# Two-layer decoder trunk on one core: the second layer's z turned by VectorE in 32x32 blocks, and a new walk of its output product

## The reference, cut to what matters

```
def conformer_mixer(hn, w_in, b_in, w_dw, b_dw, ln_g, ln_b, w_out, b_out):
    proj = hn @ w_in
    ab = proj[..., :2 * CONV_WIDTH] + b_in
    z = proj[..., 2 * CONV_WIDTH:]
    a, g = jnp.split(ab, 2, axis=-1)
    u = a * jax.nn.sigmoid(g)
    u = depthwise causal convolution of u over rows, 31 taps, + b_dw
    u = jax.nn.silu(layer_norm(u, ln_g, ln_b))
    return (u * jax.nn.silu(z)) @ w_out + b_out
```

## Time and profile before

| what | value |
|---|---|
| median of 3 runs | 853.53 us (853.16 to 853.54) |
| profiled execution, its own time | 853.52 us |
| its span in the trace | 851.5 us |
| busy: PE, DVE, ACT, POOL | 840.6, 654.5, 427.7, 337.7 us |
| granted TensorE clock, mean | 0.995 of full |
| read from memory | 156.94 MB, 187 GB/s over the span |

### The profile page before, as it was taken

One profiled execution on the slowest core, in us unless ns is written; L12 is line 12 of the kernel. 1 busy time (PEld: TensorE's weight loads), 2 busy tenths in 40 slices (PEclk: granted clock), 3 DMA queues, 4 the chain that ended last, 5 costly groups with the idle time before them and its releaser, 6 DMA issues.

```text
span 851.5 us, 12154 instructions
## 1 busy us (share of the span) xinstructions
PE 840.6 (99%) x3909; PEld 698.0 (82%) x3909; DVE 654.5 (77%) x1143; ACT 427.7 (50%) x592; POOL 337.7 (40%) x169
## 2 busy tenths in 40 slices
PE   8999999999999999999999999999999999999996
PEld 6888888888888888888888788888888888888884
DVE  4688678876889688877656629999999999566555
ACT  5744544454444644454455575445444554574441
POOL 0343005500441004500000298888888878772000
PEclk9999999999999999999999999999999999999998
DMA  9956556655666556645655465555555546556532
GB/s 325 300 158 206 162 168 197 195 153 167 191 200 194 154 157 198 216 148 200 208 189 196 146 198 195 176 177 195 194 169 181 196 152 197 194 208 239 196 98 99
DMA packets 97509, 159.49 MB, mean 187 GB/s; under 512 B 3300, under 2 KB 38468, under 8 KB 97092
## 3 DMA queue, kind: packets, MB, share of 16 engines
q1 hardware_dynamic: 97284, 158.97, 57.7%
q10 hardware_dynamic: 192, 0.08, 0.0%
HBM read 156.94 MB, written 2.10 MB: 187 GB/s over the span
## 4 chain that ended last, share of the span: by engine, by line
PE 97%; issue 1%; DMA 0%; DVE 0%; ACT 0%; DVEq 0%; POOLq 0%; POOL 0%; ACTq 0%
PE acc L419 29%; PE acc L421 29%; PE acc L420 29%; PE X L429 2%; PE acc L404 1%; PE acc L406 1%; PE acc L405 1%; PE acc L485 1%; PE acc L500 1%; PE X L550 1%; DMA ident<-in_identity 0%; PE X L559 0%; PE X L544 0%; PE X L543 0%; PE X L560 0%
## 5 line engine op out<-in xcount | busy, mean ns | idle before, releaser
L772 ACT ACTIVATE w_hi<-raw 128x1024 fp32r<-128x1024 f32 x282 | 298.9, 1061 | 359.8 <-PE acc L421 359.3
L419 PE MATMUL acc<-w_hi,xT_hi 128*128 128x512 f32 x864 | 339.6, 393 | 0.0
L421 PE MATMUL acc<-w_hi,xT_lo 128*128 128x512 f32 x864 | 336.6, 390 | 0.0
L420 PE MATMUL acc<-w_lo,xT_hi 128*128 128x512 f32 x864 | 336.2, 389 | 0.0
L1058 DVE TENSOR_TENSOR w_lo<-raw,w_hi 128x1024 fp32r<-128x1024 f32 x182 | 243.8, 1350 | 95.5 <-ACT w_hi L772 93.5
L1490 POOL TENSOR_TENSOR w_lo<-raw,w_hi 128x1024 fp32r<-128x1024 f32 x100 | 243.0, 2436 | 49.1 <-ACT w_hi L772 48.8
L421 PEld LDWEIGHTS acc<-w_hi,xT_lo 128*128 128x128 f32 x864 | 162.2, 188 | 34.0
L419 PEld LDWEIGHTS acc<-w_hi,xT_hi 128*128 128x128 f32 x864 | 162.3, 188 | 32.9 <-DVE xT_lo L1077 0.3
L420 PEld LDWEIGHTS acc<-w_lo,xT_hi 128*128 128x128 f32 x864 | 162.4, 188 | 32.6
L1315 DVE SCALAR_TENSOR_TENSOR X<-u_pad,taps,X 128x256 f32<-128x256 f32 x464 | 182.6, 480 | 0.0
L1453 POOL TENSOR_TENSOR small<-small 128x1 f32<-128x1 f32 (+1 forms) x7 | 4.3, 616 | 231.3 <-DVE small L1261 124.0
(11 more groups left out here) (150 smaller groups left out, 731.6 us busy)
## 6 DMA issues: line engine op xcount, KB each, us to landing
raw<-in_w_in SPq DMA_DIRECT2D x78, 1024.0 KB, 5.3
raw<-in_w_in SPq DMA_DIRECT2D x66, 512.0 KB, 4.4
raw<-in_w_out SPq DMA_DIRECT2D x32, 1024.0 KB, 5.0
gpost<-in_post_g SPq DMA_DIRECT2D x2, 1024.0 KB, 4.6
xrow<-in_x SPq DMA_DIRECT2D x4, 256.0 KB, 5.5
raw<-in_w_in SPq DMA_DIRECT2D x4, 256.0 KB, 4.8
xrow<-in_x SPq DMA_DIRECT2D x2, 512.0 KB, 9.5
bout<-in_b_out SPq DMA_DIRECT2D x1, 1024.0 KB, 7.0
```

Of the source, the lines that this page charges most:

```text
L419: nc.tensor.matmul(a, hi[:, k, rows], w_hi[:, slot, i], start=(k == 0), stop=False)
L420: nc.tensor.matmul(a, hi[:, k, rows], w_lo[:, slot, i], start=False, stop=False)
L421: last = nc.tensor.matmul(a, lo[:, k, rows], w_hi[:, slot, i], start=False, stop=(k == KT - 1))
L772: nc.scalar.activation(w_hi[:, slot], raw[:, u % LOADS, 2 * half:2 * half + 2], ACT.Copy).then_inc(hi_ready[slot], 1)
```

## The change

- `gate_T` and `GATE_AT` are gone. DVE turns z_row1 into a new tile `zT` in SBUF with `turn_gate`: 4 steps of 4 block transposes for each of 4 blocks. They are placed by hand among the statistics, the normalising and the gates.
- `gate` becomes one instruction of 128x1024 per block that reads cT and zT.
- The output product walks `OUT1_ORDER`: column blocks 0 and 1 over parts 0 to 3, then by turns parts 4 and 5, then 6 and 7, then blocks 2 and 3. A part is two k tiles, so vT block 2 is first needed at slice 8 and block 3 at slice 12. Bias, gain and squares of blocks 0 and 1 move with it.
- `final_high` of the four blocks stands after ACT's slices 0, 2, 5, 9 in place of 0, 2, 4, 6 (`FINAL_AT`).
- POOL makes the low parts of slices 0 to 9 in place of 0 to 7 (`OUT1_POOL`).
- `zT` takes the place of c_row; the post gain and the output bias are loaded into the place of xT_lo, once the z product is done, in place of that of z_row1.

```diff
--- before.py
+++ after.py
@@ -54,7 +54,6 @@
 NVEC = 5 * KT
 ROOT_AT = 27
 STAT_AT = 25
-GATE_AT = (26, 28, 30)
 ROWS_AT = (7, 9, 11, 23)
 LEAD = 2
 
@@ -71,6 +70,12 @@
 OUT0_ORDER = tuple([(0, i) for i in range(6)] + [(1, i) for i in range(6)] + [(0, 6), (0, 7), (1, 6), (1, 7)]
                    + [(n, i) for n in (2, 3) for i in range(SLICES)])
 OUT0_LAST = (13, 15, 23, 31)
+OUT1_ORDER = tuple([(n, i) for n in (0, 1) for i in range(4)] + [(n, k + i) for k in (4, 6) for n in (0, 1)
+                                                              for i in (0, 1)]
+                   + [(n, i) for n in (2, 3) for i in range(SLICES)])
+OUT1_LAST = (13, 15, 23, 31)
+OUT1_POOL = 10
+FINAL_AT = (0, 2, 5, 9)
 TURN_Q, TURN_K = 15, 24
 SCORES_AT = 26
 DW_ROWS = TAPS * KT // 4
@@ -114,8 +119,9 @@
         c_row = at("c_row", B, [P, MT, D])
         z_row1 = at("z_row1", B + 16 * KB, [P, MT, D])
         y1 = at("y1", B, [P, MT, D])
-        gpost1 = at("gpost1", B + 16 * KB, [P, D])
-        bout = at("bout", B + 24 * KB, [P, D])
+        zT = at("zT", B, [P, KT, SEQ])
+        gpost1 = at("gpost1", A + 16 * KB, [P, D])
+        bout = at("bout", A + 24 * KB, [P, D])
         Dr = 144 * KB
         q_row = at("q_row", Dr, [P, MT, NCOL])
         k_row = at("k_row", Dr + 4 * KB, [P, MT, NCOL])
@@ -376,10 +382,11 @@
                 for j in range(4):
                     load(S_Z, n, 8, j, w_in1[0], n * NCOL + 2 * D)
             for j in range(16):
-                load(S_OUT1, 0, 32, j, w_out1[0], (j // 4) * NCOL)
+                n, part = OUT1_ORDER[2 * j]
+                load(S_OUT1, 0, 32, j, w_out1[0], n * NCOL, part // 2)
                 if j == 5:
 
-                    sp.wait_ge(zT_done, NG)
+                    sp.wait_ge(w_used[RING - 1], rounds(S_OUT1, 0, 0, -1))
                     sp.dma_start(gpost1[:], post_g[1:2].to_broadcast([P, D])).then_inc(bcast1_in, 16)
                     sp.dma_start(bout[:], b_out[0:1].to_broadcast([P, D])).then_inc(bcast1_in, 16)
             ov = out.rearrange("b (m p) n -> p (b m) n", p=P)
@@ -699,15 +706,6 @@
                                                 start=True, stop=True)
                 last.then_inc(stat_ready, 1)
 
-            def gate_T(n):
-
-                pe.wait_ge(rows_out, 28 + n + 1)
-                if n:
-                    pe.wait_ge(t_ready, n)
-                for b in range(2):
-                    last = pair_T(z_row1, X[2 + b], 4 * n + 2 * b)
-                last.then_inc(zT_done, 1)
-
 
             for s in range(4 * SLICES):
                 if s % SLICES == 0:
@@ -719,19 +717,16 @@
                     conv_rows(ROWS_AT.index(s))
                 if s == STAT_AT:
                     statistics_wide()
-                if s in GATE_AT:
-                    gate_T(GATE_AT.index(s))
 
 
             for s in range(4 * SLICES):
-                if s % SLICES == 0:
-                    acc_free(32 + s // SLICES)
-                if s < SLICES and s % 2 == 0:
-                    pe.wait_ge(vlo_ready, s // 2 + 1)
+                n, part = OUT1_ORDER[s]
+                if part == 0:
+                    acc_free(32 + n)
+                if n == 0 and part % 2 == 0:
+                    pe.wait_ge(vlo_ready, part // 2 + 1)
                 if s < 4 * SLICES - RING:
-                    slice_products(S_OUT1, 0, 0, s, vT_hi, vT_lo)
-                if s == 1:
-                    gate_T(NG - 1)
+                    slice_products(S_OUT1, 0, 0, s, vT_hi, vT_lo, (n, part))
 
             def last_products(m):
 
@@ -1033,14 +1028,14 @@
 
             for s in range(4 * SLICES):
                 high(S_OUT1, 0, 0, s)
-                if s in (0, 2, 4, 6):
-                    final_high(s // 2)
+                if s in FINAL_AT:
+                    final_high(FINAL_AT.index(s))
                 if s == 3:
                     block_rows(S_Z, 0, 0, 31, z_row1[:, :, 3 * NCOL:4 * NCOL], rms[2], ACT.Silu)
                 if s in (1, 3):
                     affine_silu(2 + s // 2)
-                if s % SLICES == 4 and s > SLICES:
-                    out1_squares(s // SLICES - 1)
+                if s in (18, 20, 28):
+                    out1_squares((18, 20, 28).index(s))
             out1_squares(NG - 1)
 
 
@@ -1331,7 +1326,8 @@
                         conv_tap(h * 2 + c, c, k, h * per_pair + 2 * k - 1 + c)
 
 
-            for n in range(NG):
+            def row_stats(n):
+
                 for m in range(MT):
                     if n == NG - 1:
                         dve.wait_ge(cR_done, MT * n + m + 1)
@@ -1340,6 +1336,19 @@
                         dve.wait_ge(c_ready, MT * n + m + 1)
                         rows = c_row[:, m, n * NCOL:(n + 1) * NCOL]
                     nc.vector.bn_stats(bn[:, m, n], rows).then_inc(bn_ready, 1)
+
+            def turn_gate(n, steps):
+
+                if steps[0] == 0:
+                    dve.wait_ge(rows_out, 28 + n + 1)
+                for a in steps:
+                    turn(zT[:, 4 * n:4 * n + 4], z_row1[:, :, n * NCOL:(n + 1) * NCOL], a, zT_done)
+
+            for n in range(NG - 1):
+                row_stats(n)
+            dve.wait_ge(bn_ready, MT * (NG - 1))
+            turn_gate(0, (0, 1))
+            row_stats(NG - 1)
             dve.wait_ge(bn_ready, MT * NG)
             for m in range(MT):
                 nc.vector.bn_aggr(mv[:, m], bn[:, m]).then_inc(mv_ready, 1)
@@ -1358,11 +1367,9 @@
             def gate(n):
 
                 dve.wait_ge(silu_ready, n + 1)
-                dve.wait_ge(zT_done, n + 1)
-                for b in range(2):
-                    part = cT[:, 4 * n + 2 * b:4 * n + 2 * b + 2]
-                    last = nc.vector.tensor_tensor(part, part, X[2 + b][:].rearrange("p (t r) -> p t r", t=2), ALU.mult)
-                last.then_inc(t_ready, 1)
+                dve.wait_ge(zT_done, 4 * (n + 1))
+                c = cT[:, 4 * n:4 * n + 4]
+                nc.vector.tensor_tensor(c, c, zT[:, 4 * n:4 * n + 4], ALU.mult).then_inc(t_ready, 1)
 
             def final_low(n):
 
@@ -1370,17 +1377,24 @@
                 nc.vector.tensor_tensor(vT_lo[:, 4 * n:4 * n + 4], cT[:, 4 * n:4 * n + 4],
                                         vT_hi[:, 4 * n:4 * n + 4].bitcast(f32), ALU.subtract).then_inc(vlo_ready, 1)
 
+            turn_gate(0, (2, 3))
+            turn_gate(1, (0,))
             normalise(0)
             normalise(1)
+            turn_gate(1, (1, 2))
             gate(0)
             normalise(2)
+            turn_gate(1, (3,))
             gate(1)
             final_low(0)
             normalise(3)
+            final_low(1)
+            turn_gate(2, range(4))
             gate(2)
-            final_low(1)
+            turn_gate(3, (0,))
+            final_low(2)
+            turn_gate(3, (1, 2, 3))
             gate(3)
-            final_low(2)
             final_low(3)
 
             def out1_biased(n, m):
@@ -1391,7 +1405,7 @@
                     else:
                         dve.wait_ge(row1_done, 1)
                 else:
-                    dve.wait_ge(w_used[RING - 1], rounds(S_OUT1, 0, 0, 8 * n + 7))
+                    dve.wait_ge(w_used[OUT1_LAST[n] % RING], rounds(S_OUT1, 0, 0, OUT1_LAST[n]))
                 if n == 0:
                     dve.wait_ge(bcast1_in, 32)
                 c = slice(n * NCOL, (n + 1) * NCOL)
@@ -1403,13 +1417,14 @@
                 c = slice(n * NCOL, (n + 1) * NCOL)
                 nc.vector.tensor_tensor(yg1[:, m, c], y1[:, m, c], gpost1[:, c], ALU.mult).then_inc(yg_ready, 1)
 
-            for s in range(SLICES, 4 * SLICES):
+            for s in range(OUT1_POOL, 4 * SLICES):
                 low(S_OUT1, 0, 0, s)
-                if s % SLICES == 3:
+                if s in (17, 19, 27):
+                    n = (17, 19, 27).index(s)
                     for m in range(MT):
-                        out1_biased(s // SLICES - 1, m)
+                        out1_biased(n, m)
                     for m in range(MT):
-                        out1_gained(s // SLICES - 1, m)
+                        out1_gained(n, m)
             mean_but_last(30, 4)
             out1_biased(NG - 1, 0)
             out1_gained(NG - 1, 0)
@@ -1504,7 +1519,7 @@
                 if s == ROOT_AT:
                     inverse_root(rstd, var_eps, m_half, var_ready, 1, rstd_ready)
                 low(S_Z, 0, 0, s)
-            for s in range(SLICES):
+            for s in range(OUT1_POOL):
                 low(S_OUT1, 0, 0, s)
             for m in range(MT):
                 inverse_root(rms[3][:, m:m + 1], mean_sq[:, m:m + 1], m_half[:, m:m + 1], ms_ready, 5 + m, rms_ready)
```

## The result

The changed kernel takes 854.71 us (median of 11 runs, 853.25 to 856.81) against 853.45 us before (11 runs): the ratio is 1.0023, with a 95% interval of 1.0015 to 1.0031. The forecast was 854.4. The profiled execution took 854.35 us, its span is 852.6.

The account below looks back on a forecast made before the run. PE, busy 840.6 of 851.5 us, was taken to bound the kernel; -3.56 (bursts) + 3.4 (slice 0) + 0.7 (slice 6) + 0.4 (clock) = +0.9 gave 854.4 us, range 850.3 to 856.4.

Parts of the forecast that it names:

- The bursts: Four bursts of z transposes taken off PE around the start of the output product, 0.89 us each: -3.56 us.
- The wait at slice 0: Output product's start: PE waits for the first vT_lo, which DVE makes after POOL's low part: +3.4 us.
- The hidden work: DVE's turns (1.8 us each) before the statistics, gates, moved loads and new walk: mostly no cost to PE.
- These two cost nothing and save 2.1: POOL making the low parts of output product slices 8 and 9: no cost, 2.1 us saved.
- The wait at slice 6 and the clock: Output product: PE waits 0.7 us for POOL's slice 6 low part; a clock fall adds 0.4 behind it.
- I take L = 1.1: Loss from the clock's fall around the slice 0 wait: 1.1 us, of which slice 6's wait absorbs 0.7.
- -0.2 plus the larger of L and 0.7: Whole change against the kernel before: the sum for a given clock loss L, +3.2 us with L = 2 x 1.7.
- Rival 1: After the slice 0 wait the low clock lasts double or comes twice: 855.9 to 856.7 us, chance 0.20.
- Rival 2: DVE's turns take 1.9 us or more each, so slices 0 and 6 come later: 855.0 to 856.0, chance 0.11.
- Rival 3: Gate and vlo don't lose their turn to POOL; only 0.5 us wait at slice 0: 850.5 us, chance 0.19.

Follow-up runs that it names:

- e4: Changed kernel with z block 0 turned by TensorE in one burst and DVE's turns of blocks 1 to 3 rearranged; 850.48 us, ratio 0.9969 to the kernel before.
- e2: Changed kernel with z turned by TensorE again in four bursts and the gate reading PSUM, all else kept; 853.46 us, ratio 1.0001 to the kernel before.
- e3: Changed kernel with POOL's low part of output product slice 2 made to wait for DVE's first vT_lo; 851.93 us, ratio 0.9985 to the kernel before.
- e8: As e3, with POOL waiting ahead of slice 1, twelve POOL low parts, DVE's turns reordered, silus and final highs moved; 852.29 us, ratio 0.9991 to the kernel before.
- e6: Changed kernel with POOL making the low parts of eight output product slices instead of ten; 857.97 us, ratio 1.0057 to the kernel before.
- run b: Second of three repeat profiles of the unedited changed kernel; 857.31 us.
- e5: Changed kernel with the old walk of the output product and final highs after slices 0, 2, 4, 6; 863.87 us, ratio 1.0128 to the kernel before.
- runs a and c: First and third of three repeat profiles of the unedited changed kernel; 853.15 and 854.56 us.
- e1: Changed kernel with 13 idle products on TensorE ahead of slice 0 of the output product; 854.02 us, ratio 1.0007 to the kernel before.

## Why the prediction was right

Forecast were +0.9 us and 854.4. The medians differ by 1.3 us and R by 1.5; the mean of the 11 runs is 1.9 above that of before, because five of them form an upper group (855.93 to 856.81).

**The bursts** (-3.56): right. e4 saves three of them and its R falls by 2.7, e2 puts them back and nothing remains.

**The wait at slice 0** (+3.4): right in size, place and cause. 3.42 with the restart; the chain on DVE came within 0.1 us of the forecast at vT_lo. Of these 3.4 us about 2.2 are POOL's turn at the lock; the other 1.26, which e3 leaves, go when no turn stands between normalise 0 and the first vT_lo (e4). POOL was ahead of vT_lo by 0.11 us, as forecast (0.1), and the prediction itself says that this could have fallen the other way; it came out alike in every profile that has this order.

**The hidden work:** turns at 1.81 us, two of them free before the statistics, gates at 1.24, 1.40, 1.39 and 2.50 us (forecast 1.5, 1.6, 1.2 and 2.8), loads and walk at nothing (e2). The gate does wait for POOL: gate 0 ended 1.08 us after POOL's low part, as vT_lo had ended 1.09 us after one before, and gate 2 took 3.42 us in e8. The Trainium skill (SBUF — State Buffer, Who interferes with whom) says that a DVE instruction with two SBUF inputs contends with a GpSimd instruction that reads SBUF; these traces agree. "These two cost nothing and save 2.1" was right in kind: without them the wait at slice 8 is 2.4 (e6).

**The wait at slice 6 and the clock** (+0.7 and +0.4 behind it): here is the term that was mis-sized. "I take L = 1.1" (L is the time lost to the low clock) should have been 1.6, since the low stretch began 1.2 us after PE was back and lay wholly over products; it then covered the whole of the wait at slice 6. By the prediction's own formula, -0.2 plus the larger of L and 0.7, the sum is +1.4 and the time 854.9, where 854.7 was measured. It had been within the bounds given.

**The rivals.** Rival 1 is not what the median shows, but it is real: run b has the double stretch (L = 6.0 x 0.467 = 2.8, a sum of +2.6, where R shows +2.7), and e5 has it twice. Five of the 11 runs of the changed kernel lie at its price, 855.9 to 856.7, or within 0.1 us of it, at a mean clock of 0.992 to 0.994 where the others have 0.996; none of the five was profiled, so how much of that is the clock and how much the start is open. The median stands at the top of the lower six, so one run more in the upper group would have put it at 855.9: that the forecast came so close is luck in part. Rival 2 fell (1.81 us a turn). Rival 3 fell: the lock did hold vT_lo back; e3, which takes that away from the first vT_lo, gains 2.9 us in R.

## What to carry to other kernels

Work taken off the bounding engine comes back as a wait if it lands on a neighbour in front of something the bounding engine needs; count what of it lies ahead of the first need, and move only what fits (here three blocks of four). Where two engines share a lock, a wait that holds the less urgent one back can gain time (2.2 us here). And a wait on PE has to be priced with the low stretch of the clock behind it: with 3.2 us of wait went 1.6 us in three of the four profiles of the changed kernel and 2.8 in the fourth.

## What the runs showed of the hardware

The fall of the clock doesn't come with every wait of the same length: after 3.16 to 3.19 us at slice 0 it came in five profiles of the six without filler and not in e6's, where it came after 2.38 us at slice 8; after waits of 1.0 and 1.8 us it didn't come (e3, e8). Where PE still waited when it came (run b, e5) the clock was low for 6.8 us, some 5.9 of them over products; where it came 0.3 us (e6) or 1.1 to 1.2 us (the profile above, runs a and c) after PE was back, for 3.4 us. The Trainium skill (TensorE: Matmul & The Clock Gate, Why this matters for your kernels) warns that idle gaps between bursts of matmuls bring the clock down. Five of these six profiles agree, the sixth doesn't at slice 0. With idle products on a zero tile in the wait the clock stayed at full in the one profile taken (e1).

At the lock between DVE and POOL the one whose instruction started first went first in the meetings read here, by 0.11 us in the changed kernel and 0.06 in e8, and the other's instruction then took a whole one of the first's longer (3.38 us in place of 1.21, 3.42 in place of 1.22). The gate that reads z from PSUM wasn't held: in e4 gate 0 ran from 741.75 to 743.03, 1.28 us for its two instructions, though POOL's low part was at work until 742.23.
